# Half of the cached latents turned by transfers within SBUF and VectorE block transposes, with spaced gathers, one rotary product, and another start and end

## The chip, the cores and the metric

One core of one Trainium2 chip runs the whole program in one launch. The metric is the device time in microseconds (us); the number of the kernel before is the median of three runs. A profiled execution of the same program, with a trace of every instruction, is a run of its own with a time of its own.

## What is computed

A decoder trunk of two layers for one prompt of 256 tokens and for 8 sequences that add one token each. The 264 tokens share the weights, so they go through every projection together. Each layer has three branches (gated delta rule, latent attention, mLSTM), a merge and a feed-forward block with a short convolution; a last RMSNorm ends it. The part that the change touches most is the latent attention of the 8 sample sequences over 2048 cached positions each:

```python
q_lat = jnp.einsum('bqhd,chd->bqhc', q_nope, w_uk.reshape(MLA_KV_LORA, MLA_HEADS, MLA_NOPE))
s_past = jnp.einsum('bqhc,bkc->bhqk', q_lat, lat_past) + jnp.einsum('bqhr,bkr->bhqk', q_rope, kr_past)
...
p = jax.nn.softmax(s, axis=-1).astype(lat_past.dtype)
ctx = (jnp.einsum('bhqk,bkc->bqhc', p[..., :past], lat_past)
       + jnp.einsum('bhqk,bkc->bqhc', p[..., past:], c_kv.astype(lat_past.dtype)))
...
y_prompt = rmsnorm(xp, final_norm_g)
y_sample = rmsnorm(xs, final_norm_g)
```

`lat_past` (2048 rows of 128 latents a sequence) and `kr_past` (2048 rows of 32) are gathered through a page table. Everything is float32.

## The kernel before

**Program.** Five engines have streams written out by hand, one function each (sync, tensor, scalar, vector, gpsimd), and wait for one another by semaphores. TensorE's order is the plan: `schedule()` lists every PSUM bank's product in that order and who reads it ("A" ScalarE, "V" VectorE), and the other streams must follow it.

**Weight stream.** SyncE loads the weights in units of 512 KB into a ring of 8 slots (`ring`, line 500). It may issue unit u once TensorE has started unit u - 7 of that count (`w_started`). A unit feeds 8 tiles of 128x128; `weights` (line 547) multiplies each by 264 token columns.

**Pieces.** Projections whose results are needed late (`PIECES`, half a unit each, 4 tiles) fill TensorE's stream while other engines work on the branches: `half(n)` does the next n of them on TensorE, and the same calls in ScalarE's and VectorE's streams evacuate those that are complete. They use two of the eight PSUM banks in turn, so a piece waits for the evacuation of the one before last.

**Pages.** `pages(n)` handles sequence n = 0 to 7 of a layer. `lat[n]` holds its 2048 cached rows, 16 of 128 latents in each partition (1 MB); `key[n]` the rotary keys. Per page:
- TensorE turns the 16 blocks of `lat[n]` by transposes (line 1032) into four banks `ltr`; ScalarE copies two of them to `ltt` and VectorE the other two (line 2052), and VectorE turns `key[n]` by one block transpose (line 2049).
- One piece, then the scores: four products with the latents (line 1039) and four with the rotary keys (line 1042), each into 32 of the 128 output rows. Four pages add up in one bank `ss`.

After four pages `top(g)` finds the maximum, ScalarE takes the exponent (`powers`), `turned(g)` sums, `context(g)` multiplies the probabilities with `lat` untransposed (line 1078), and `combine(g)` (line 1089) sorts the result. Pages 4 to 7 are placed between these steps of group 0.

**Gathers.** GpSimd issues two indirect transfers for each page (`gather`, lines 2338 and 2339). Those of pages 0 to 3 are issued earlier; those of 4 to 7 all together once `pv` is evacuated.

**Other places.** After `os`, one piece and then the products `mn0` (line 833), which wait for VectorE's `ones_column` (line 1894). `outer` (line 847) multiplies 32 rows at a time on four row groups in turn; `mout` (line 900) does so on two. At the start VectorE scales x (line 1553) once `par_loaded` has reached 80: the parameters from SyncE (16) and four tiny transfers to `prow` from ScalarE's queue (64). At the end: sum of squares over the last tile, one product with ones, root, reciprocal over 128x264 (line 2196), eight products on VectorE (line 2199), four stores.

## Time and profile before

| | us |
|---|---|
| median of 3 runs | 1277.28 (1276.53 to 1277.31) |
| profiled execution | 1287.18 |
| its span | 1285.3 |
| TensorE busy | 1258.9 |
| VectorE busy | 546.0 |
| ScalarE busy | 254.3 |
| GpSimd busy | 153.1 |
| read from and written to HBM | 183.9 and 9.3 MB |

The span is divided into what TensorE does and where it waits. The chain of waits follows the work that ended last back from release to release; most of it is TensorE's line 547. A float32 product shows as two passes in the trace, a transpose as one. The rows that matter are given below.

### The profile page before, as it was taken

The page shows a single profiled execution, that of the slowest core. Times are in us where ns is not written, and L with a number is a line of the kernel's source. Part 1 is how long each engine was busy: PE and PEld are TensorE (multiplying, and loading weights), DVE is VectorE, ACT ScalarE, POOL GpSimd, SP SyncE. Part 2 cuts the span into 40 slices and gives each one's busy share as a digit, 9 for nine tenths or more (in the row PEclk, how much of TensorE's full clock was granted, in tenths as well). Part 3 has the DMA queues.
Part 4 walks back from the last instruction along what each step waited for, and adds up shares of the span by engine and source line. Part 5 has one row for each costly group of instructions (what it writes and reads, how often), then busy time and mean ns, then how long its engine had stood idle before and what let it go on. Part 6 is the DMA issues. An engine that isn't in the chain of part 4 may idle for free.

```text
span 1285.3 us, 18245 instructions
## 1 busy us (share of the span) xinstructions
PE 1258.9 (98%) x7278; PEld 1027.3 (80%) x7278; DVE 546.0 (42%) x1372; ACT 254.3 (20%) x648; POOL 153.1 (12%) x210
## 2 busy tenths in 40 slices
PE   7999999999999999999999999999999999999997
PEld 6878777677888888888888787786788888888885
DVE  7975646332135333331178846553311353334212
ACT  3432325222000111110033224342210011111000
POOL 2012442200000000020001035412000000000000
PEclk9999999999999999999999999999999999999999
DMA  9433476522444444464444344745234444444440
GB/s 336 153 99 102 132 249 226 214 82 83 132 153 147 148 148 148 147 218 151 147 152 137 109 129 145 259 164 213 67 99 147 152 145 149 149 149 148 153 133 34
DMA packets 59603, 194.30 MB, mean 151 GB/s; under 512 B 7824, under 2 KB 8112, under 8 KB 56704
## 3 DMA queue, kind: packets, MB, share of 16 engines
q1 hardware_dynamic: 50544, 152.22, 36.6%
q0 software_dynamic: 8768, 40.84, 8.9%
q8 instruction: 58, 0.95, 0.3%
q14 instruction: 25, 0.20, 0.0%
q10 hardware_dynamic: 208, 0.09, 0.0%
HBM read 183.86 MB, written 9.25 MB: 150 GB/s over the span
## 4 chain that ended last, share of the span: by engine, by line
PE 93%; DVE 3%; issue 2%; ACT 1%; POOL 0%; another core or an unknown queue 0%; DMA 0%; ACTq 0%; DVEq 0%; POOLq 0%
PE banks L547 75%; PE banks L1032 3%; PE banks L1039 1%; PE banks L1042 1%; PE banks L938 1%; PE banks L1078 1%; DVE arena L1658 1%; PE banks L966 1%; PE banks L691 1%; PE banks L847 0%; PE banks L982 0%; PE banks L564 0%; DMA arena<-in_par 0%; POOL arena L2282 0%
## 5 line engine op out<-in xcount | busy, mean ns | idle before, releaser
L547 PE MATMUL banks<-arena 128*128 128x264 f32 x4512 | 1032.1, 388 | 7.4 <-DVE arena L1553 6.7
L547 PEld LDWEIGHTS banks<-arena 128*128 128x128 f32 x4512 | 850.7, 190 | 171.8 <-issue 14.3
L1167 ACT ACTIVATE arena<-banks 128x256 f32<-128x256 f32 (+8 forms) x260 | 96.9, 397 | 436.0 <-PE banks L547 293.6
L2153 DVE TENSOR_SCALAR arena<-arena 128x256 f32<-128x256 f32 x44 | 18.2, 414 | 129.9 <-ACT arena L1167 129.7
L2186 DVE SCALAR_TENSOR_TENSOR arena<-banks,arena 128x264 f32<-128x264 f32 x16 | 6.9, 433 | 135.0 <-PE banks L547 135.0
L2364 POOL COPY arena<-arena 128x2 f32<-128x2 f32 x44 | 13.6, 310 | 377.7 <-ACT arena L1167 276.0
L1747 DVE SCALAR_TENSOR_TENSOR arena<-arena,banks 128x264 f32<-128x264 f32 x16 | 6.9, 430 | 73.6 <-PE banks L547 73.6
L1198 ACT ACTIVATE arena<-banks 128x264 f32<-128x264 f32 x32 | 12.5, 391 | 127.4 <-PE banks L547 127.4
L1032 PEld LDWEIGHTS banks<-arena 128*128 128x128 f32 x256 | 28.8, 145 | 7.4 <-issue 7.3
L2052 DVE COPY arena<-banks 128x512 f32<-128x512 f32 x32 | 21.5, 679 | 28.5 <-PE banks L1032 15.7
L1032 PE MATMUL banks<-arena 128*128 128x128 f32 x256 | 32.1, 280 | 0.0
L1479 ACT ACTIVATE arena<-arena 128x256 f32<-128x256 f32 x44 | 18.4, 417 | 66.4 <-DVE arena L2155 66.4
L2160 DVE SCALAR_TENSOR_TENSOR arena<-arena 128x256 f32<-128x256 f32 x44 | 18.7, 426 | 26.8 <-ACT arena L1479 26.6
L2360 POOL DMA_DIRECT2D arena<-in_ffn x2 | 2.9, 1432 | 225.4 <-ACT arena L1167 225.4
L2165 DVE TENSOR_TENSOR arena<-arena,banks 128x256 f32<-128x256 f32 x42 | 17.7, 422 | 26.8 <-PE banks L547 26.6
L2338 POOL DMA_INDIRECT arena<-in_lat,page_row x16 | 15.4, 961 | 88.8 <-ACT arena L1167 67.6
L1039 PE MATMUL banks<-arena 128*32 128x512 f32 x128 | 18.3, 643 | 6.8 <-ACT arena L1167 6.3
L1658 DVE SCALAR_TENSOR_TENSOR arena<-arena 128x256 f32<-128x256 f32 x48 | 23.3, 485 | 1.7
L2155 DVE SCALAR_TENSOR_TENSOR arena<-arena 128x256 f32<-128x256 f32 x44 | 21.5, 490 | 1.6
L2154 DVE SCALAR_TENSOR_TENSOR arena<-arena 128x256 f32<-128x256 f32 x44 | 21.4, 485 | 1.5
L2122 DVE SCALAR_TENSOR_TENSOR arena<-banks,arena 128x264 f32<-128x264 f32 x16 | 6.9, 432 | 34.9 <-PE banks L547 34.9
L2262 POOL TENSOR_TENSOR arena<-arena 128x512 f32<-128x512 f32 x16 | 16.1, 1038 | 37.2 <-DVE arena L1813 37.2
(435 smaller groups left out, 1042.9 us busy)
## 6 DMA issues: line engine op xcount, KB each, us to landing
arena<-in_weights SPq DMA_DIRECT2D x230, 512.0 KB, 3.5
arena<-in_weights SPq DMA_DIRECT2D x112, 256.0 KB, 3.0
arena<-in_s POOLq DMA_DIRECT2D x2, 2048.0 KB, 11.0
out_ss_o<-arena POOLq DMA_DIRECT2D x16, 256.0 KB, 3.0
arena<-in_mla_w POOLq DMA_DIRECT2D x4, 1024.0 KB, 6.8
arena<-in_c POOLq DMA_DIRECT2D x4, 512.0 KB, 5.8
out_sc_o<-arena POOLq DMA_DIRECT2D x16, 128.0 KB, 3.5
arena<-in_x SPq DMA_DIRECT2D x4, 264.0 KB, 5.2
```

Of the source, the lines that this page charges most:

```text
L547: mm = nc.tensor.matmul(dst, ring[:, at_:at_ + 128], rhs[:, j, :], start=(start and j == 0), stop=(stop and j == k - 1))
L1032: mm = nc.tensor.transpose(b[:, q * P:(q + 1) * P], lat[n][:, r_ * P:(r_ + 1) * P], ident)
L1039: nc.tensor.matmul(heads(sb[32 * i:32 * i + 32, :], 32), ql_pad[:, g, s_, :], turned_lat(n)[:, :, 32 * i:32 * i + 32], start=(s_ == 0), st ...
L1167: return A(dst, src, ACT.Copy, scale=scale)
L1479: A(fth[:, j % 3, :], fcv[:, j % 3, :], ACT.Tanh, scale=0.5).then_inc(*up("ffn_tanh"))
L1658: link(stt(cv, ci[:, j, 24 + t:24 + t + TP], w[t], cv, ALU.mult, ALU.add))
L2052: V.tensor_copy(ltt[:, n % 2, i, :], bank("ltr", 4 * n + i)).then_inc(*read("ltr", 4 * n + i))
L2153: link(ts(cv, fc[:, j % 3, 0:TP], w[0], par[:, Q_FB + j:Q_FB + j + 1], ALU.mult, ALU.add))
L2154: link(stt(cv, fc[:, j % 3, 1:1 + TP], w[1], cv, ALU.mult, ALU.add))
L2155: stt(cv, fc[:, j % 3, 2:2 + TP], w[2], cv, ALU.mult, ALU.add).then_inc(*up("ffn_conv"))
L2160: link(stt(cv, fth[:, j % 3, :], 1.0, cv, ALU.add, ALU.mult))
L2165: tt_(hid[:, j, 0:TP], cv, bank("fu", j)[:, 0:TP], ALU.mult)
```

## The change

1. **Latents of sequences 4 to 7.** Their turning leaves TensorE. `lat[n]` is copied into `lat[n - 4]` (free once `context(0)` has read it) by 16 transfers within SBUF for each page, of 32 partitions x 16 x 32 elements (`quarter_of_latents`): 128-byte runs, which swap the four 32-partition groups with the four 32-latent groups. Then VectorE turns each 512 columns by a block transpose of 32x32 blocks, four a page. SyncE issues pages 4 and 6, at two places of the weight stream (`BLOCKS_AT`), ScalarE pages 5 and 7, four transfers ahead of each of eight `half(1)`.
2. **Order.** Pages 4 to 7 follow `combine(0)` and 11 pieces. One more piece stands ahead of `mn0`.
3. **Gathers.** Page 4's is issued as before; those of 5, 6 and 7 each after the transposes of page 1, 2 and 3.
4. **Rotary product.** `qr_pad` is laid out with all heads' 128 columns, so that one product replaces four.
5. **`mout`** uses four row groups; `kvt` and `vd` are filled for all 128 rows by two more products.
6. **Start.** The first unit is loaded in two halves, x's first part on ScalarE's queue, and `par_loaded` no longer includes `prow`.
7. **End.** Sums of squares of all tokens as columns (128x3) by small products, root and reciprocal on these, spread by products into two banks; x was scaled by the gain earlier; VectorE does five tiles and stores go out from SyncE, GpSimd does three tiles and ScalarE issues their stores.

```diff
@@ schedule @@
-    add("mkT", 2); add("mvT", 2); add("sk", 1, "V"); add("mqk", 2, "V"); add("os", 1, "V"); half(1)
+    add("mkT", 2); add("mvT", 2); add("sk", 1, "V"); add("mqk", 2, "V"); add("os", 1, "V"); half(2)
...
@@ sync @@
+            def blocks_of_latents(l, n):
+                sp.wait_ge(*out(l, "cx", 0))
+                sp.wait_ge(*at(l, f"lat_in{n}", 32))
+                for b in range(4):
+                    for q in range(4):
+                        sp.dma_start(*quarter_of_latents(n, b, q)).then_inc(*up(f"lat_blocks{n}", 16))
...
+                if u % UNITS in (BLOCKS_AT, BLOCKS_AT + 1):
+                    blocks_of_latents(u // UNITS, 4 + 2 * (u % UNITS - BLOCKS_AT))
...
+        def quarter_of_latents(n, b, q):
+
+            return (lat[n - 4][32 * q:32 * q + 32, 512 * b:512 * b + 512].rearrange("i (r j) -> i r j", r=NR),
+                    lat[n][32 * b:32 * b + 32, :].rearrange("i (r q j) -> i r q j", r=NR, q=4)[:, :, q, :])
@@ tensor, pages @@
+                    half(1)
+                    if n < 4:
...
+                    else:
+                        pe.wait_ge(*at(l, "lat_turned", 4 * (n - 3)))
...
-                    for i in range(4):
-                        mm = nc.tensor.matmul(sb[32 * i:32 * i + 32, :], qr_pad[:, i, g, s_, :], krt[:, n % 2, :],
-                                              start=False, stop=(s_ == 3), skip_group_check=True)
+                    mm = nc.tensor.matmul(sb, qr_pad[:, g, s_, :], krt[:, n % 2, :], start=False, stop=(s_ == 3), skip_group_check=True)
@@ scalar @@
+                for n in (5, 7):
+                    act.wait_ge(*at(l, f"lat_in{n}", 32))
+                    for b in range(4):
+                        for q in range(4):
+                            nc.scalar.dma_start(*quarter_of_latents(n, b, q)).then_inc(*up(f"lat_blocks{n}", 16))
+                        half(1)
@@ vector, pages @@
+                    else:
+                        dve.wait_ge(*at(l, f"lat_blocks{n}", 256))
+                        for i in range(4):
+                            V.transpose(ltt[:, n % 2, i, :], lat[n - 4][:, 512 * i:512 * i + 512]).then_inc(*up("lat_turned"))
@@ gpsimd @@
-                for n in range(4, NB):
+                gather(4)
+                for n in range(5, NB):
+                    pool.wait_ge(*out(l, "ltr", 4 * (n - 4) + 3))
+                    plain()
                     gather(n)
@@ end of the tensor stream @@
-            pe.wait_ge(last_sum, 7)
-            nc.tensor.matmul(banks[:, 0, 0:TT], ones, nsum, start=True, stop=True).then_inc(last_total, 1)
+            tokens = [slice(0, P), slice(P, TP), slice(TT - P, TT)]
...
+            for b in last_rms:
+                for i, s in enumerate(tokens[:2]):
+                    nc.tensor.matmul(b[:, s], roots[:, i:i + 1].to_broadcast((P, P)), ident, start=True, stop=True, skip_group_check=True)
```

TensorE's stream of layer 1 before, from page 4's transposes to page 6's (L1032 transposes, L547 pieces at 4 products each, L1039 and L1042 scores, L1068 `turned`, L1078 `context`):

```order
L1032 MATMUL banks<-arena 128x128 x16
L547 MATMUL banks<-arena 128x264 x4
L1039 MATMUL banks<-arena 32x512 x4
L1042 MATMUL banks<-arena 32x512 x4
L547 MATMUL banks<-arena 128x264 x4
L1068 MATMUL banks<-arena 128x1
L1032 MATMUL banks<-arena 128x128 x16
L547 MATMUL banks<-arena 128x264 x4
L1039 MATMUL banks<-arena 32x512 x4
L1042 MATMUL banks<-arena 32x512 x4
L1078 MATMUL banks<-arena 32x128 x64
L1032 MATMUL banks<-arena 128x128 x16
```

The same stretch of the changed kernel, from the pieces after `top(0)` to page 5 (L567 pieces, L1095 `turned`, L1105 `context`, L1116 `combine`, L1068 and L1070 scores):

```order
L567 MATMUL banks<-arena 128x264 x12
L1095 MATMUL banks<-arena 128x1
L1105 MATMUL banks<-arena 32x128 x64
L567 MATMUL banks<-arena 128x264 x8
L1116 MATMUL banks<-arena 128x8 x4
L567 MATMUL banks<-arena 128x264 x48
L1068 MATMUL banks<-arena 32x512 x4
L1070 MATMUL banks<-arena 128x512
L567 MATMUL banks<-arena 128x264 x4
L1068 MATMUL banks<-arena 32x512 x4
L1070 MATMUL banks<-arena 128x512
```

The transposes are gone, three, two and twelve pieces stand around `context(0)` and `combine(0)`, and pages 4 to 7 follow one after another.

SyncE's queue of the changed kernel around the two places of the transfers (L518 weights, L501 transfers of pages 4 and 6); before, these were 34 half units in a row:

```order
L518 DMA arena<-in_weights 128x512 x8
L501 DMA arena<-arena 32x16x32 x16
L518 DMA arena<-in_weights 128x512 x2
L501 DMA arena<-arena 32x16x32 x16
L518 DMA arena<-in_weights 128x512 x24
```

Every weight unit behind them waits for `context(0)` and for their issue.

ScalarE's stream of the changed kernel from the exponent of group 0 (L1474) through the copy of the context (L1206), with the transfers of pages 5 and 7 (L1493) between evacuations of pieces (L1237):

```order
L1474 ACTIVATE arena<-banks,arena 128x512
L1237 ACTIVATE arena<-banks 128x264 x2
L1206 ACTIVATE arena<-banks,arena 128x512
L1493 DMA arena<-arena 32x16x32 x8
L1237 ACTIVATE arena<-banks 128x264
L1493 DMA arena<-arena 32x16x32 x8
L1237 ACTIVATE arena<-banks 128x264
L1493 DMA arena<-arena 32x16x32 x8
L1237 ACTIVATE arena<-banks 128x264
L1493 DMA arena<-arena 32x16x32 x8
```

Eight transfers now stand ahead of each of four evacuations.

## Rows read from the trace of the kernel before

**Rows 1.** The page, busy time, share of the span and instructions of each engine
```profile
PE 1258.9 (98%) x7278; PEld 1027.3 (80%) x7278; DVE 546.0 (42%) x1372; ACT 254.3 (20%) x648; POOL 153.1 (12%) x210
```
**Rows 2.** Waits of TensorE: line, released by; us in total, times, longest
```profile
PE banks L547 <- DVE arena L1553: 6.7, 1, 6.7
PE banks L1039 <- ACT arena L1167: 6.3, 2, 3.2
PE banks L833 <- DVE arena L1894: 2.5, 2, 1.2
```
**Rows 3.** Chain of waits, pages 1 to 3 of layer 1: start, us, what
```profile
247.16 3.09 PE banks L1032 x16
...
256.84 2.63 PE banks L1032 x16
...
263.14 1.90 PE banks L1032 x16
265.04 1.78 PE banks L547 x8
266.82 1.02 PE banks L1039 x8
267.84 0.86 PE banks L1042 x8
```
**Rows 4.** Timeline of TensorE, then ScalarE, at page 1: start, us, engine, line
```profile
247.09 1.97 PE L1032 MATMUL banks<-arena 128*128 128x128 f32 x16
...
250.27 0.60 ACT L1167 ACTIVATE arena<-banks 128x512 f32<-128x512 f32 x1 [6.58 <-PE banks L1032]
253.15 0.60 ACT L1167 ACTIVATE arena<-banks 128x512 f32<-128x512 f32 x1 [2.28 <-remote]
```
**Rows 5.** Timeline of GpSimd, first and last of eight gathers
```profile
241.68 0.95 POOL L2338 DMA_INDIRECT arena<-in_lat,page_row  x1 [33.78 <-ACT arena L1167]
...
250.47 0.95 POOL L2339 DMA_INDIRECT arena<-in_key,page_row  x1 [0.30 <-issue]
```
**Rows 6.** Stretch 250 to 260: busy by engine, granted clock, DMA share, GB/s
```profile
250.00:260.00 10.00, 6.84 (x40) 4.07 (x39) 3.52 (x6) 2.39 (x4) 1.12 (x2) 0.83 0.85 349
```
**Rows 7.** VectorE's block transposes: ns min/median/max, first and last start
```profile
L2049 DVE STREAM_TRANSPOSE arena<-arena x16: 687/702/711, 242.0 to 930.7; 128x512 f32<-128x512 f32 x16
```
**Rows 8.** DMA queues (packets, MB, share) at 364:371, 2.3:6.5, all; weight issues; landing
```profile
q0 software_dynamic: 64, 0.18, 15.6%
...
q10 hardware_dynamic: 24, 0.00, 0.3%
...
q1 hardware_dynamic: 50544, 152.22, 36.6%
...
L500 SPq DMA_DIRECT2D arena<-in_weights x342: 327/328/1521, 1.7 to 1246.9; - x171
...
arena<-in_weights SPq DMA_DIRECT2D x112, 256.0 KB, 3.0
```
**Rows 9.** Chain of waits at the outer products of the delta rule and of mLSTM
```profile
152.47 1.07 PE banks L847 x8
...
177.06 1.92 PE banks L900 x8
```
**Rows 10.** Chain of waits at the start and at the end
```profile
2.16 4.07 DMA arena<-in_par
...
6.66 6.73 PE banks L547 x16
...
1254.90 20.14 PE banks L547 x90
...
1277.66 1.81 DVE arena L2196
...
1280.40 2.42 DVE arena L2199 x6
```
**Rows 11.** The page, a group of GpSimd: busy, mean ns of one, idle before
```profile
L2262 POOL TENSOR_TENSOR arena<-arena 128x512 f32<-128x512 f32 x16 | 16.1, 1038 | 37.2 <-DVE arena L1813 37.2
```

More of the change, by code:

```diff
@@ L494, in _ @@
                 if u == 1:
-                    for i in range(1, 4):
+                    for i in range(2, 4):
                         load_x(i)
@@ L543, in weights @@
                         slot = unit % SLOTS
-                        if part == 0:
+                        if unit == 0 and part == 0:
+                            pe.wait_ge(first_half, 16)
+                        elif part == 0 or unit == 0 and part == 4:
                             pe.wait_ge(w_landed[slot], landed[unit])
@@ L1096, in _ @@
                 top(0)
-                pages(4)
-                half(1)
+                half(3)
                 turned(0)
-                pages(5)
                 context(0)
-                pages(6)
-                half(1)
+                half(2)
                 combine(0)
-                pages(7)
+                half(11)
+                for n in range(4, NB):
+                    pages(n)
                 half(2)
@@ L1325, in _ @@
                 A(dm, dm, ACT.Exp, scale=-1.0).then_inc(*up("mdecay_exp"))
-                half(1)
+                half(2)
                 act.wait_ge(*out(l, "mn0"))
@@ L1347, in _ @@
                 act.wait_ge(*out(l, "out", 7))
-                copy(kvt[0:64, :], bank("mkvT")[0:64, 0:P]).then_inc(*read("mkvT"))
+                copy(kvt, bank("mkvT")[:, 0:P]).then_inc(*read("mkvT"))
                 half(3)
@@ L1447, in _ @@
                 powers(0)
-                pages(4)
-                half(1)
-                pages(5)
+                half(3)
                 context(0)
-                pages(6)
-                half(1)
-                pages(7)
+                for n in (5, 7):
+                    act.wait_ge(*at(l, f"lat_in{n}", 32))
+                    for b in range(4):
+                        for q in range(4):
+                            nc.scalar.dma_start(*quarter_of_latents(n, b, q)).then_inc(*up(f"lat_blocks{n}", 16))
+                        half(1)
+                half(5)
+                half(4)
                 half(3)
@@ L2091, in _ @@
                 top(0, 1)
-                pages(4)
-                half(1)
+                half(3)
                 total(0)
-                pages(5)
                 newest(0)
-                pages(6)
-                half(1)
+                half(2)
                 combined(0)
-                pages(7)
+                half(11)
+                for n in range(4, NB):
+                    pages(n)
                 top(1, 2)
@@ L2383, in _ @@
                 close()
+            pool.wait_ge(last_copy, 1)
+            pool.wait_ge(last_scaled, KT)
+            for k in range(5, KT):
+                tt_(hn[:, k, :], raw[:, k, :], rms, ALU.mult).then_inc(last_pool, 1)
         assert not [n for n in SIGNALS if given[n] != L * SIGNALS[n]], given
```

144 lines of the change are left out of this document (87 added, 57 removed).

## The prediction

> **What bounds the kernel now.** I read the page's busy times first: TensorE is busy for 98% of the span [rows 1], so a time that falls off TensorE's stream, or a gap in it that closes, is a gain, and work that moves to another engine costs only where TensorE comes to wait for it. Then the waits of TensorE by who released it [rows 2]: 6.7 us at the start, 6.3 in two waits before page 1's score products, 2.5 in two waits before the products of line 833. The chain of waits then gives the price of every piece of the stream, and the stretches where TensorE itself shows no wait but runs long.
>
> **The profiled execution is not the timed one.** It takes 1287.18 us (span 1285.3), the timed runs 1277.28: 9.9 us apart. The chain shows a place of about that size. An undisturbed page is 1.90 us of transposes, 1.78 of projection, 1.02 and 0.86 of scores, 5.56 in all [rows 3]. Page 1 of layer 1 runs from 247.16 to 256.84, 9.68, and page 2 from there to 263.14, 6.30: 4.86 us too much, and the second wait of the pair [rows 2] stands in layer 2 in the same place, so some 9.7 us in both. What happens there: TensorE's transposes of page 1 start at 247.09, but ScalarE's copy of the first of them is released only at 250.27 and the next at 253.15 by nothing that the profile can name [rows 4]. It is not the data of those transposes that is missing, since they have run. It falls together with eight gathers issued back to back from 241.68 to 250.47 [rows 5], with 349 GB/s on the DMA engines, and the granted clock sinks to 0.83 of the stretch, in part at the 1.2 GHz level, after TensorE's gap [rows 6]. The signal of a finished product arrives late while the memory is saturated. The recording itself may cause that delay, since it has every product to note down just then. That 9.9 and 9.7 agree is my reason to give this the larger chance: the timed runs then have no such stall, and spacing the gathers gains 9.7 us in the profile and nothing in the timed runs. The Trainium skill ("NOTIFIC — the notification-queue block", section 7.1) says that the recorder's inner pipeline holds its producer back rather than lose a record and that the path could throttle an engine; no row here shows that counter, and by that rule the gain would be of the profile alone.
>
> **The change part by part, in timed microseconds.**
>
> *Transposes of pages 4 to 7 off TensorE.* Per layer four groups of 16, 1.80 to 1.90 each (as the row of page 3, 1.90 [rows 3]); 4 x 1.85 x 2 layers = 14.8 gained. They become 16 VectorE block transposes of 128x512 a layer in the place of 8 copies of the same size, each 0.70 [rows 7], and 64 transfers a layer.
>
> *When are they needed?* Call T0 the end of context(0) (the 128 passes of line 1078 in the chain of before). After it TensorE has 2 + 11 pieces, at 20.14/90 x 8 = 1.79 us each [rows 10], some 0.8 of combine, and page 4's own piece: page 4's scores are due at T0 + 26. VectorE reads piece 12 of these at T0 + 22.3, then needs 0.9 for it and 5 transposes x 0.70: done at about T0 + 26.7. So TensorE waits some 0.5 us for page 4, and hardly for pages 5 to 7 (a page takes TensorE 1.79 + 1.9, VectorE 3.5, with two buffers): 1.0 lost in both layers. Page 6's and 7's blocks must have landed by T0 + 31.
>
> *The transfers.* A layer has 64 x 512 = 32768 pieces of 128 bytes, 2048 for each of 16 DMA engines. No row of before has such a transfer. Below: the load of in_ffn is 2816 pieces of 64 bytes in 64 packets; 15.6% of 16 engines x 7 us is 17.5 us, 6.2 ns a piece [rows 8], so 12.7 us a layer. Above: every piece a packet of its own. A packet of 4 to 16 bytes costs 0.3% x 16 x 4.2 us / 24 = 8.4 ns, and bytes cost 36.6% x 16 x 1285.3 us / 152.22 MB = 49 ns per KB, 6.3 for 128 bytes [rows 8]: 14.7 ns, 30.1 us a layer. I take 13, 26.6 us, close to the dear end: q10, of the tiny packets, is ScalarE's queue, which the change uses, and in_ffn comes through GpSimd's. With 3 us for the landing and the two weight units queued between them, all is there by T0 + 30, just within T0 + 31: nothing lost, and at 14.7 ns 2 us a layer. The weight stream behind them on SyncE: units up to seven ahead have been issued, the eighth is needed at T0 + 36. In general a layer loses 2048 p + 3 - 31 us, p the price of a piece.
>
> The Trainium skill speaks both ways ("DMA: Bandwidth & Descriptors"). Its table of specifications has at least 512 bytes for line rate, with a read-modify-write below that; a doubled 14.7 ns would lose 32 us a layer. Its section "Why small descriptors are slow" exempts transfers within SBUF and has 128-byte packets at 78% of link rate, by which a layer's 4 MB would take an estimated 12 us. No row shows either.
>
> *Issuing.* ScalarE issues 32 of these in a layer between evacuations that free the two banks of the pieces. If an issue takes i, its fourth evacuation stands at 32 i + 2.3 and the bank is wanted at T0 + 17: no wait up to 0.46. A weight load, 128 rows, takes 0.328 [rows 8]; if that doesn't depend on the rows, 0.33; if it is all by row, 4 x 0.328 = 1.31 for 512. I take the low end, the row that is nearest in kind, and 0.
>
> *Spaced gathers.* 0 timed, 9.7 in the profile (above); bounds 0 and 9.7.
>
> *A further piece before the products of line 833.* The wait there, 2.5 in two [rows 2], is shorter than the piece (1.79) put ahead of each: 2.5 gained. What is late next: nothing, since the piece is taken from a place with no wait.
>
> *Outer products on four row groups.* L900 with two row groups takes 1.92 for 8 passes, L847 with four 1.07 [rows 9]: 0.85 x 2 = 1.7. Four added products of 128x128 in float32, at twice a transpose's 1.90/16: 0.24 x 4 = 0.9. Net 0.8.
>
> *One rotary product for four.* 8 passes in 0.86 [rows 3] become 2 of 512 columns over the full width. The four ran side by side, so the two take the same; at the rate of the other score rows, 1.02, it would be 16 x 0.16 = 2.6 worse. I take 0.
>
> *Start.* The first product at 6.66 waits for VectorE, which waits for the last of four tiny parameter transfers, issued 2.16 and landed 6.23 [rows 10]. It now waits for the first of them only, for x from ScalarE's queue and for half a weight unit: a 256 KB half lands in 3.0 [rows 8] and is issued near 1.3, so the first product may stand at 4.5. The 16 passes that follow take 6.73, 0.42 each, nearly twice 20.14/90, so they keep their length and move. Gain 2.0; between 0.5, if x's later tiles are late, and 2.3.
>
> *Tail.* From the last pass, 1275.04, to 1285.3 it is 10.3 us: three VectorE steps, a product, a root, a reciprocal over 264 columns of 1.81, eight products of which six take 2.42 up to 1282.8 [rows 10], and 2.5 for the last store. After: two VectorE steps 0.95, small products 0.4, root and reciprocal of three columns 0.4, spreading 0.5, then five products of 0.40 on VectorE beside a copy and three on GpSimd (0.4 + 3 x 0.6, from 1.04 for 512 columns [rows 11]), store 2.5: 7.2. Gain 3.0 (2 to 4).
>
> Sum: 14.8 - 1.0 + 2.5 + 0.8 + 2.0 + 3.0 = 22.1. Timed 1277.28 - 22.1 = **1255**. In the profile 9.7 more: span 1285.3 - 31.8 = 1253.5, about the timed value.
>
> **Rivals.** *B: the stall at page 1 is in the timed runs too.* For it: the late signals stand in the trace with all consequences, clock included. Against: the 9.9 us. It gives 1277.28 - 31.8 = 1245.5. *C: small losses around the blocks.* Issue at 0.6 instead of 0.33 leaves ScalarE 32 x 0.6 + 2.3 - 17 = 4.5 us late a layer, 9 in all: 1264; pieces of 15 to 18 ns give 6 to 18 likewise. For it: deadlines with margins of 1 us. *D, slower than before: the price of a piece.* TensorE stands before page 4's and page 6's scores, and behind the blocks on SyncE's queue the weights. It takes back all 22.1 when 2048 p - 28 = 11, p = 19 ns; at 25 ns it loses 23.2 a layer and the time is 1255 + 46 = 1301. Against it: a 14.7 ns bound put together from the dearest rows; for it: neither row is a transfer from SBUF to SBUF through 32 partitions. ScalarE's issues reach the same point at i = 0.81.
>
> **How the numbers follow.** Forecast (1250 to 1259) 0.48; B (1241 to 1249) 0.22; C (1259 to 1274) 0.15; D 0.11; between C and D, 1274 to 1280, 0.04. The range leaves out D, what lies between and the ends: 1242 to 1272. A measurement of this kernel can tell some 0.2%, 2.5 us: faster 0.86, same 0.03, slower 0.11.
>
> **What would show it.** In the profile of the changed kernel: 128 transposes on TensorE's transpose line instead of 256; page 1 in 5.6 us; no wait at mn0's products; mout's 8 passes in about 1.07; the first product near 4.5 and 7 us from the last pass of the stream to the end; ScalarE's issues at 0.33 to 0.45; the blocks' packets at 13 ns and landed 26 to 30 us after context(0); timed and profiled times within 3 us. A wait of TensorE longer than 1 us before page 4 to 7's scores, or at a piece for weights, refutes the price of the pieces; a profile that stays 10 us above the timed runs refutes the reading of page 1.

## The result: 1300.5 us, slower by 23.5, and the profile after

The changed kernel takes 1300.51 us (median of 1299.38 to 1301.65), the kernel before beside it 1277.04 (1276.53 to 1277.31): a ratio of 1.0183, 95% interval 1.0171 to 1.0195. I had forecast 1255, with a range of 1242 to 1272. The time lies in my rival D, but the price of a piece, D's main mechanism, is not what put it there.

The page of the changed kernel, first row, then the two queues of SyncE and of ScalarE (packets, MB, share of 16 engines):

```profile
PE 1258.9 (97%) x7084; PEld 1024.7 (79%) x7084; DVE 551.7 (42%) x1392; ACT 245.8 (19%) x633; POOL 155.4 (12%) x213
q1 hardware_dynamic: 84192, 155.74, 40.3%
q10 hardware_dynamic: 34432, 4.96, 3.5%
```

TensorE is busy for as many microseconds as before [rows 1], although 128 transposes are gone; slow passes, below, fill their place. Half of the 65536 new packets are on q1, half on q10. TensorE's waits (line, released by; us in total, times, longest) say where it lost:

```profile
PE banks L567 <- ACT arena L1237: 15.3, 4, 4.2
PE banks L567 <- issue: 7.1, 2, 4.6
PE banks L567 <- DMA arena<-in_weights: 5.0, 1, 5.0
PE banks L930 <- DVE arena L2004: 1.5, 2, 0.7
PE banks L1068 <- DVE arena L2109: 1.2, 4, 0.4
```

The two waits of page 1 and those of line 833 [rows 2] are gone, the one at the start is shorter (5.0 for 6.7). New are 22.4 us at line 567, the pieces of projection, three waits a layer, and 1.5 at line 930. The blocks themselves cost 1.2: TensorE hardly ever waits for the scores. In time, TensorE in layer 1 from the end of context(0), 277.5:

```profile
277.39 3.83 PE L567 MATMUL banks<-arena 128*128 128x264 f32 x16
...
281.87 7.37 PE L567 MATMUL banks<-arena 128*128 128x264 f32 x32
292.54 3.83 PE L567 MATMUL banks<-arena 128*128 128x264 f32 x16 [3.31 <-ACT arena L1237]
300.97 3.70 PE L567 MATMUL banks<-arena 128*128 128x264 f32 x8 [4.60 <-issue]
308.63 12.11 PE L567 MATMUL banks<-arena 128*128 128x264 f32 x40 [3.96 <-ACT arena L1237]
321.17 1.06 PE L1068 MATMUL banks<-arena 128*32 128x512 f32 x8 [0.42 <-DVE arena L2109]
```

And ScalarE in the same stretch (L1493 issues a transfer, L1237 reads a finished piece and frees its bank):

```profile
277.53 6.56 ACTq L1493 DMA_DIRECT2D arena<-arena  x8
284.14 0.39 ACT L1237 ACTIVATE arena<-banks 128x264 f32<-128x264 f32 x1 [5.92 <-issue]
284.15 7.89 ACTq L1493 DMA_DIRECT2D arena<-arena  x8
292.10 0.39 ACT L1237 ACTIVATE arena<-banks 128x264 f32<-128x264 f32 x1 [7.57 <-issue]
292.12 8.31 ACTq L1493 DMA_DIRECT2D arena<-arena  x8
300.48 0.39 ACT L1237 ACTIVATE arena<-banks 128x264 f32<-128x264 f32 x1 [7.99 <-issue]
300.50 7.64 ACTq L1493 DMA_DIRECT2D arena<-arena  x8
308.19 0.39 ACT L1237 ACTIVATE arena<-banks 128x264 f32<-128x264 f32 x1 [7.32 <-issue]
```

The two rows of starts interlock. ScalarE reads a piece at 292.10, TensorE goes on at 292.54; ScalarE at 300.48, TensorE at 300.97; 308.19 and 308.63. Between 277.5 and 308.2 ScalarE does nothing but issue, apart from its copy of the context and three reads. One issue lasts 0.95 us on average there (30.4 / 32). What follows each wait is slow too. The stretches by 10 us (busy of TensorE, its weight loads, VectorE, ScalarE, GpSimd; granted clock; DMA share, which passes 1 where packets of two queues overlap; GB/s):

```profile
290.00:300.00 10.00, 3.83 (x16) 2.96 (x16) 0.00 (x0) 0.39 (x1) 0.00 (x0) 1.00 1.49 163
300.00:310.00 10.00, 5.07 (x11) 3.68 (x12) 0.86 (x2) 0.78 (x2) 0.00 (x0) 0.72 1.56 145
310.00:320.00 10.00, 10.00 (x36) 8.02 (x36) 2.75 (x6) 0.39 (x1) 0.00 (x0) 0.77 1.14 292
```

After a stretch in which TensorE was busy for 3.83 of 10 us, the granted clock is 0.72 and then 0.77, so part of these 20 us ran at the 1.2 GHz level. Forty passes take 12.11 where 40 x 20.14 / 90 [rows 10] is 8.95, eight take 3.70 for 1.79: 5.1 us a layer, on top of 11.9 of waits (3.31 + 4.60 + 3.96). Layer 2 shows the same (waits of 3.74, 2.47 and 4.25, together 10.5, and 6.9 of slow passes).

The other places. A page is now (chain of waits: start, us, what; compare [rows 3]):

```profile
247.38 1.75 PE banks L1057 x16
249.13 1.78 PE banks L567 x8
250.91 1.02 PE banks L1068 x8
251.93 1.06 PE banks L1070 x2
...
177.13 1.15 PE banks L924 x8
```

The last row is the outer products, 1.15 for 1.92 [rows 9]. The end of the kernel, from the last pass at 1285.38:

```profile
1287.43 0.18 DVE L2252 RECIPROCAL arena<-arena 128x3 f32<-128x3 f32 x1 [0.86 <-ACT arena L1534]
1287.67 1.22 PE L1174 MATMUL banks<-arena 128*128 128x128 f32 x4 [0.48 <-DVE arena L2252]
1289.45 1.79 DVE L2255 TENSOR_TENSOR arena<-arena,banks 128x264 f32<-128x264 f32 x5 [1.83 <-PE banks L1175]
1291.59 2.14 POOL L2446 TENSOR_TENSOR arena<-arena 128x264 f32<-128x264 f32 x3 [85.83 <-ACT arena L1536]
```

It is 14.5 us from the last pass to the end of the span, 1299.9; it was 10.3. E2, with the same code at the end, has 13.0. The 1.5 between them is the clock: the products that spread the roots (L1174 here) ran at a granted clock of 0.50 from 1287.9 to 1289.9, and at 1.00 in E2:

```profile
1267.08 0.71 PE L1165 MATMUL banks<-arena 128*128 128x128 f32 x4 [0.48 <-DVE arena L2236]
```

### The profile page after: what moved, and what is told of

It is laid out like the page before. It is cut to its first block, busy times and chain, and to the rows that moved or that the text cites. A ratio compares the mean times of both kernels' runs of the same rounds, so it can differ in the third digit from the quotient of the medians.

```text
span 1299.9 us, 17990 instructions
## 1 busy us (share of the span) xinstructions
PE 1258.9 (97%) x7084; PEld 1024.7 (79%) x7084; DVE 551.7 (42%) x1392; ACT 245.8 (19%) x633; POOL 155.4 (12%) x213
## 4 chain that ended last, share of the span: by engine, by line
PE 88%; ACTq 4%; DVE 4%; issue 1%; ACT 1%; DMA 0%; SPq 0%; POOL 0%; POOLq 0%; DVEq 0%
PE banks L567 72%; ACTq L1493 4%; PE banks L1070 1%; PE banks L1105 1%; PE banks L1068 1%; PE banks L1057 1%; PE banks L962 1%; DVE arena L2109 1%; DVE arena L1710 1%; PE banks L990 1%; PE banks L711 1%; PE banks L669 0%; DMA arena<-in_x 0%; PE banks L1006 0%; DVE arena L2004 0%
## 5 line engine op out<-in xcount | busy, mean ns | idle before, releaser
L567 PE MATMUL banks<-arena 128*128 128x264 f32 x4512 | 1044.5, 391 | 28.0 <-ACT arena L1237 15.3
L567 PEld LDWEIGHTS banks<-arena 128*128 128x128 f32 x4512 | 857.9, 192 | 197.4 <-issue 21.9
L1206 ACT ACTIVATE arena<-banks 128x256 f32<-128x256 f32 (+8 forms) x244 | 87.7, 384 | 389.2 <-PE banks L567 292.9
L1799 DVE SCALAR_TENSOR_TENSOR arena<-arena,banks 128x264 f32<-128x264 f32 x16 | 6.9, 430 | 99.6 <-PE banks L567 99.6
L1237 ACT ACTIVATE arena<-banks 128x264 f32<-128x264 f32 x32 | 12.5, 391 | 177.8 <-PE banks L567 120.0
L1794 DVE SCALAR_TENSOR_TENSOR arena<-arena,banks 128x264 f32<-128x264 f32 x16 | 6.9, 429 | 30.3 <-PE banks L567 30.3
L2109 DVE STREAM_TRANSPOSE arena<-arena 128x512 f32<-128x512 f32 x32 | 19.6, 671 | 0.0
L2105 DVE COPY arena<-banks 128x512 f32<-128x512 f32 x16 | 11.1, 692 | 18.9 <-PE banks L1057 18.9
L1068 PE MATMUL banks<-arena 128*32 128x512 f32 x128 | 17.2, 610 | 1.2 <-DVE arena L2109 1.2
```

What stands on the lines that cost most here:

```text
L567: mm = nc.tensor.matmul(dst, ring[:, at_:at_ + 128], rhs[:, j, :], start=(start and j == 0), stop=(stop and j == k - 1))
L1068: nc.tensor.matmul(heads(sb[32 * i:32 * i + 32, :], 32), ql_pad[:, g, s_, :], turned, start=(s_ == 0), stop=False, skip_group_check=True)
L1206: return A(dst, src, ACT.Copy, scale=scale)
L2109: V.transpose(ltt[:, n % 2, i, :], lat[n - 4][:, 512 * i:512 * i + 512]).then_inc(*up("lat_turned"))
```

## The experiments

Sixteen experiments on four chips. Beside them the kernel before takes 1283.9 to 1288.1 us in every one of 36 executions, not 1277; E1 bears on that. So I compare mostly kernel with kernel. E3, E5, E6 and E9 leave transfers out or copy other shapes, so that their output is another, and have one execution each; the others have four to ten.

**E1, the gathers alone**

```diff
-                for n in range(4, NB):
+                gather(4)
+                for n in range(5, NB):
+                    pool.wait_ge(*out(l, "ltr", 4 * (n - 4) + 3))
+                    plain()
                     gather(n)
```

> The kernel before with one edit: the last three pairs of gathers of a layer wait for TensorE's transposes of pages 1, 2 and 3, as in the changed kernel. Theory (the stall at page 1 belongs to the recorded execution): in the trace page 1 takes about 5.6 us instead of 9.68, the span falls by some 9.7 us to about 1275.6, and the timed runs do not move: 1277 within 1.5 us, so that profiled and timed execution agree within 2 us. Rival B (the stall is in every execution): the timed runs fall to about 1267.5.

Measured: 1276.89 (1276.62 to 1277.28), before 1285.82 beside it, ratio 0.9934 (0.9917 to 0.9950); span 1274.7. Page 1 in its trace:

```profile
247.97 1.95 PE L547 MATMUL banks<-arena 128*128 128x264 f32 x8
249.85 1.09 PE L1039 MATMUL banks<-arena 128*32 128x512 f32 x8
```

No wait before the scores. Spacing the gathers removes the stall, and what I expected of this kernel came: page 1 undisturbed, the span at 1274.7, the time at 1277. What I had not expected is the kernel before beside it, 1285.8 and not 1277. That could mean that the stall depends on the chip and not on the recording. But each of the 36 executions, like every execution of E1 and of the changed kernel, has a span and a granted clock of its own on record, as the profiled execution has; the four at 1276.5 to 1277.3 have neither. "A recorded execution stalls" and "these four chips stall, and the one of my prediction doesn't" both fit all of this, and no run separates them. The second needs the profiled execution behind the prediction, 1287.18, to have run on such a chip, which isn't recorded.

**E13, the changed kernel again**, beside the kernel before on such a chip

> The changed kernel as it is, timed beside the kernel before on a chip of the experiments, where the kernel before took 1286 to 1287 and not 1277. Theory (before's stall at page 1 is in its timed runs on these chips, and the changed kernel has no such stall anywhere): 1300 as before, so the loss here is 13 to 15 us instead of 23.5. Rival (these chips are slower for every kernel by 0.7%): 1309.

Measured: 1299.64 (1297.72 to 1301.49) against 1287.04: ratio 1.0095 (1.0079 to 1.0110). The changed kernel takes what it took (1300.51), so these chips are not slower for every kernel; the loss is 12.6 us against executions of the kernel before at 1287, and 23.5 against those at 1277.

**E2, everything but the blocks** (pages 4 to 7 turned by TensorE in their old places, no transfers within the chip, all other hunks of the change)

> The changed kernel without its main part: pages 4 to 7 are turned by TensorE where they were before, no blocks are transferred; the gathers, the rotary product, the further piece, the outer products on four row groups, the start and the tail are as in the changed kernel. Theory (the blocks cost all of the loss, and the smaller edits give less than I took): start -1.0, the wait at line 833 -2.5, outer products +1 to +2, rotary product 16 x 0.2 less what the transposes give back, 0 to +3.2, tail +3.7 by what the two traces show, gathers 0: 1277 to 1282. The blocks then carry 18 to 24 of the 23.5 us. Rival (the smaller edits are worth what I predicted, -8.3): 1269, and the blocks carry 31. Rival (they are themselves the loss): above 1290.

Measured: 1279.98 (1279.90 to 1280.15), 3.1 above E1 and within the expected 1277 to 1282. The rest of the change, for which I had 8.3 of gain, loses 3.1; the blocks lose 19.7 (1299.6 - 1280.0), where I had 13.8 of gain.

**E3, pages 5 and 7 left out**

```diff
-                    act.wait_ge(*at(l, f"lat_in{n}", 32))
                     for b in range(4):
-                        for q in range(4):
-                            nc.scalar.dma_start(*quarter_of_latents(n, b, q)).then_inc(*up(f"lat_blocks{n}", 16))
                         half(1)
```

> The changed kernel without ScalarE's 32 transfers a layer (the blocks of pages 5 and 7 are left out, VectorE transposes what lies in their buffers, so the output for sequences 5 and 7 is another). SyncE still issues its 32. Theory (an issue lasts as long as the DMA engines need to take up its pieces, both queues sharing them at 16.2 ns a piece): SyncE's issues fall from a median of 0.90 us to 32 x 16.2 ns = 0.52, or to the 0.6 of the first ones, whichever is longer; a layer's 16384 packets are done some 18 to 20 us after context(0); no wait of TensorE is left at the pieces, and the span falls by about 2 x 17 to 1266 to 1270. Rival (an issue has a fixed price of its own, whatever else is queued): SyncE's issues stay at 0.9. Rival (the loss comes from the packets under way, not from ScalarE's issues): TensorE's waits at the pieces stay in part.

Measured: 1265.99. No wait of TensorE at the pieces is left. SyncE's issues now (ns min/median/max), and the queue in 9 us of them, 280 to 289:

```profile
L501 SPq DMA_DIRECT2D arena<-arena x64: 591/630/1551, 278.3 to 922.0; - x64
q1 hardware_dynamic: 6602, 0.82, 58.5%
```

In the changed kernel the same line has 591/900/1909. From context(0) to page 4's scores it is 26.5 us (277.52 to 304.04), in the changed kernel 43.7 (277.5 to 321.17): the 17 us a layer. SyncE's issues fell with ScalarE's gone, so an issue has no fixed price of 0.9. A piece costs 58.5% x 16 x 9 / 6602 = 12.8 ns here. The gain of the transposes is whole: 1280.0 - 1266.0 = 14.0.

**E6, pages 4 and 6 left out**

```diff
-                if u % UNITS in (BLOCKS_AT, BLOCKS_AT + 1):
-                    blocks_of_latents(u // UNITS, 4 + 2 * (u % UNITS - BLOCKS_AT))
```

> The mirror of the run without pages 5 and 7: SyncE's 32 transfers a layer are left out (VectorE transposes what lies in the buffers of pages 4 and 6, so their output is another), ScalarE issues its own 32 with nothing beside them. Theory (0.71 us an issue, as SyncE's took when alone, is enough to hold ScalarE): its fourth evacuation of these comes 32 x 0.71 + 2.3 = 25 us after context(0) where TensorE wants the bank at 17: 8 us a layer, 16 in all above the 1266 of the mirror run, 1280 to 1284. Rival (ScalarE is late only since both queues together fill the DMA engines): no wait at the pieces, 1266 to 1269.

Measured: 1291.85. ScalarE's issues, and TensorE's waits:

```profile
L1491 ACTq DMA_DIRECT2D arena<-arena x64: 607/657/1928, 277.6 to 937.7; - x64
PE banks L565 <- ACT arena L1235: 9.5, 4, 3.4
PE banks L565 <- issue: 7.6, 2, 3.9
```

ScalarE's fourth read of a piece comes 25.6 us after context(0) (25 expected). The waits are 17.1 (16 expected). What I left out again is the clock: the whole is 25.9 above E3, so some 9 us follow from the slow passes after the waits (granted clock 0.53 from 300 to 310). Issues of 0.66 us in the median and 0.79 on average (25.4 / 32) are enough to lose 25.9 of the 33.6 us, with half of the pieces and only SyncE's weight loads beside them.

**E5, the same transfers in pieces of 2 KB**

```diff
-            return (lat[n - 4][32 * q:32 * q + 32, 512 * b:512 * b + 512].rearrange("i (r j) -> i r j", r=NR),
-                    lat[n][32 * b:32 * b + 32, :].rearrange("i (r q j) -> i r q j", r=NR, q=4)[:, :, q, :])
+            return lat[n - 4][32 * q:32 * q + 32, 512 * b:512 * b + 512], lat[n][32 * b:32 * b + 32, 512 * q:512 * q + 512]
```

> The changed kernel with the same 64 transfers a layer, the same queues and the same 64 KB each, but each of 32 rows is copied as one piece of 2 KB instead of 16 pieces of 128 bytes (the blocks lie wrong, so the scores of pages 4 to 7 are another computation). Theory (the number of pieces sets both how long an issue lasts and how long the DMA engines work): 128 pieces an engine a layer instead of 2048, an issue of 0.35 us or less, all blocks landed about 16 us after context(0), at 49 ns a KB some 13 us of transfer; no wait of TensorE at the pieces: 1266 to 1270, as with pages 5 and 7 left out. Rival (bytes or the number of transfers decide): issues stay near 0.9 to 1.0, the time near 1300.

Measured: 1282.14.

```profile
L1492 ACTq DMA_DIRECT2D arena<-arena x64: 521/614/1775, 277.8 to 929.0; - x64
PE banks L566 <- ACT arena L1236: 7.5, 2, 4.4
PE banks L566 <- issue: 3.1, 2, 1.6
```

Half of my theory fell: a sixteenth of the pieces, and an issue still lasts 0.61. The other half held: the pieces' crowd on the DMA engines had raised it to 0.87, and without them 17.5 us of the loss go (1299.6 - 1282.1).

**E9, other shapes**

```diff
+            k = 128 * (4 * b + q) if n % 2 == 0 else 512 * b
+            return lat[n - 4][:, k:k + (128 if n % 2 == 0 else 512)], lat[n][:, k:k + (128 if n % 2 == 0 else 512)]
...
-                        for q in range(4):
+                        for q in range(1):
```

> The changed kernel with its transfers within SBUF in two other shapes (plain copies, so the scores of pages 4 to 7 are another computation): SyncE's 32 a layer copy 128 rows of 512 bytes each, 64 KB as before; ScalarE's are 8 a layer of 128 rows of 2 KB, 256 KB each, the shape of a weight load but from SBUF instead of memory. What is measured is how long an issue lasts: 32 rows as 512 pieces of 128 bytes took 0.71 alone, 32 rows of 2 KB 0.66, a weight load of 128 rows 0.33 to 0.43. Theory (it is the source within SBUF that makes an issue dear): 0.65 or more in both shapes. Rival (it is the shape, 32 rows on one side): 0.33 to 0.43 in both. With ScalarE's eight issues at either price there is no wait at the pieces: 1266 to 1269.

Measured: 1265.90, and the issues of ScalarE (128 rows of 2 KB), then of SyncE (128 rows of 512 bytes):

```profile
L1493 ACTq DMA_DIRECT2D arena<-arena x16: 472/566/1216, 277.7 to 910.9; - x16
L501 SPq DMA_DIRECT2D arena<-arena x64: 471/602/1975, 278.3 to 921.4; - x64
```

A load of weights with the same rows takes 0.33 [rows 8], and it does so in this trace too (median 328 ns, at most 725). What differs is that the source lies in SBUF: 0.57 to 0.60. So the number of rows or pieces hardly counts for the issue; whether both ends lie in SBUF does. (I had said 0.65 or more; it is a little less.) With eight issues a layer instead of 32, ScalarE delays nobody.

**E4, GpSimd issues pages 5 and 7**

```diff
+                pool.wait_ge(*out(l, "cx", 0))
+                for n in (5, 7):
+                    pool.wait_ge(*at(l, f"lat_in{n}", 32))
...
+                            dma(*quarter_of_latents(n, b, q)).then_inc(*up(f"lat_blocks{n}", 16))
```

> The changed kernel with ScalarE's 32 transfers a layer issued by GpSimd, which has nothing to do there; same transfers, same order, complete computation. From the trace of before a GpSimd issue lasts 0.52 to 0.55 us, one of 2816 pieces 1.43: some 0.7 for 512 pieces. Theory (ScalarE held by its issues is what makes TensorE wait, the pieces themselves arrive almost in time): TensorE's waits at the pieces vanish; the blocks land at context(0) + 35 at most, 1 to 4 us late a layer for pages 6 and 7: timed 1266 to 1273. If GpSimd's way of writing its packets gives 6.2 ns for a piece, as in_ffn's 64-byte pieces had, all are in by + 28 and it is 1264 to 1267. Rival (the price of the pieces is the cause, whoever issues them): 1285 or above, with TensorE waiting before the scores of pages 4 to 7 instead.

Measured: 1279.77 (1279.47 to 1281.91). TensorE's waits:

```profile
PE banks L1068 <- DVE arena L2106: 15.3, 4, 6.6
```

ScalarE was the cause of the waits at the pieces: they are gone. The rest is worse than I expected (1266 to 1273), though below the rival's 1285. GpSimd's 32 issues (0.67 each) are out in 20.6 us, and while they run SyncE's first 16 take 25.9 us; page 4, wanted first, is the one that suffers. TensorE stands 6.6 us before page 4's scores. GpSimd's transfers show on a queue of their own as packets of 2 KB (274 to 318):

```profile
q0 software_dynamic: 1024, 2.10, 39.7%
```

That is 39.7% x 16 x 44 us / 1024 = 0.27 us a packet, 17 ns for 128 bytes: no cheaper than the pieces of the other queues.

**E8, both queues in order of need** (of each page eight transfers by SyncE, eight by GpSimd, page after page)

> The changed kernel with the blocks in order of need: of each page's 16 transfers SyncE issues eight and GpSimd eight, page 4 first, GpSimd starting a page when SyncE's half of the page before has landed; ScalarE issues none. Complete computation. Theory (the DMA engines take up 512 pieces of a page in 8.3 us at 16.2 ns, and only the order and ScalarE's issues lost time): pages 4, 5, 6, 7 have landed 11, 19, 28 and 36 us after context(0), where VectorE wants them at 22 to 26, 29, 33 and 36: 1265 to 1269. Rival (the drain itself is too slow, by the same 16 to 17 ns, since GpSimd's and SyncE's transfers don't overlap well or weights behind SyncE's half come late): 1272 to 1280.

Measured: 1283.31 (1279.88 to 1286.16), above even the rival's range. The theory fell. Page 7's blocks landed 44 us after context(0), TensorE waited 7.7 us for them in one layer, and the weights behind SyncE's share came 3.7 us late. The packets of the two queues took 92% of the DMA engines' time in the 34 us from 278 (shares of 55.0 and 36.9), so there was little slack that an order could use. It is not a clean test of order, though: this kernel holds GpSimd back until SyncE's half has landed, and GpSimd stands idle for 6.5, 2.5 and 6.6 us between its groups.

**E7, the tail without GpSimd** (base: E2)

```diff
-            for k in range(5):
+            for k in range(KT):
                 tt_(hn[:, k, :], raw[:, k, :], last_rms[0], ALU.mult).then_inc(last_norm, 1)
...
-            for k in range(5, KT):
-                tt_(hn[:, k, :], raw[:, k, :], rms, ALU.mult).then_inc(last_pool, 1)
```

> The kernel with all edits but the blocks (1280.0), its last products changed: VectorE makes all eight instead of five, ScalarE's copy and GpSimd's three products go, the last store waits for VectorE. Theory (GpSimd's own end, 8.07 us from the start of its late products, ends the span, 3.7 us after the last store has landed): from the last pass to the end 9 to 9.8 us instead of 13.0, 1276 to 1277. Rival (the stores set the end, GpSimd's drain only stands beside them): three products more on VectorE, 1.0, take the place of GpSimd's 2.1, 1279 to 1280.

Measured: 1275.59 (1274.99 to 1275.82), 4.4 below E2. From the last pass to the end it is 10.0 us (1263.9 to 1273.9) instead of 13.0, though the roots were spread at a granted clock of 0.52 here; at full clock, in E10's trace, it is 9.3. Another 0.9 lies at the start, where the tiles of x happened to land earlier than in E2's trace. The trace has for the last instruction of GpSimd's program, a drain (start from the end of the span, us):

```
changed, E2, E3, E5, E6, E13:  -8.30  8.07 us     E9:  -8.31  8.08 us
E4:  -4.67  3.74 us     E8:  -4.68  4.40 us
before, E1, E7:  none of GpSimd in the last 16 us
```

In the changed kernel it runs from 1291.6 to 1299.6, 3.8 us beyond the last store's landing at 1295.8. It begins with GpSimd's three late products. Why it is shorter in E4 and E8, where GpSimd had issued 64 transfers more, I can't tell; there the stores end the span.

**E10, no blocks, and two edits undone** (base: E7 without the outer products on four row groups and without the single rotary product)

> No blocks: gathers in order, the further piece, the start, and the tail on VectorE as in the run without GpSimd; the outer products on four row groups and the single rotary product are undone. Theory (both cost time: the outer products 0.96 a layer, from the time between the products of the normalization and those of the output in the two traces, the rotary product 0.05 a page): 1275.6 - 1.9 - 0.8 = 1272.9. Rival (they are worth what I predicted, 0.8 and 0): 1276.4.

Measured: 1272.88 (1272.24 to 1273.54), 2.7 below E7, as expected. The outer products (E2, then E10; from the first product of their operands to the next stage):

```profile
173.16 0.27 PE L906 MATMUL banks<-arena 128*64 128x128 f32 x1
...
178.07 1.14 PE L919 MATMUL banks<-arena 32*128 32x512 f32 x8
...
181.92 1.97 PE L925 MATMUL banks<-arena 128*32 128x128 f32 x64 [0.73 <-DVE arena L1992]
```

```profile
172.50 0.27 PE L906 MATMUL banks<-arena 128*64 128x128 f32 x1
...
176.38 1.99 PE L915 MATMUL banks<-arena 32*128 32x512 f32 x8
...
180.27 1.97 PE L921 MATMUL banks<-arena 128*32 128x128 f32 x64
```

8.76 us against 7.77. The faster products (1.14) send TensorE into a wait for VectorE that reads their results (0.73), and the added products cost another 0.9. The rotary product was not tested by itself.

**E14, without the new start** (base: E10)

> The kernel without blocks of 1272.9, with the start as in the kernel before (one load of x and one whole unit first, VectorE waiting for all five parameter transfers). Theory (the later tiles of x decide when the first normalization is through, with either start; the steady stream began at 12.8 to 13.7 us in the traces of both): 1272.9 within 1. Rival (the new start is worth the 2.0 that I predicted): 1274.9.

Measured: 1273.23 (1272.97 to 1273.40): the start is worth 0.35, less than the four executions of E10 differ (1.3).

**E12, two pages through blocks, all by SyncE** (base: E10; pages 4 and 5 stay with TensorE)

> The same with pages 6 and 7 alone turned through blocks, all 32 transfers issued by SyncE. Complete computation. Theory: SyncE alone needs 23 us for them at 0.71 us an issue, with no wait of TensorE, as in the run without pages 5 and 7: 4 groups of 1.85 less, 7.4, less 0.5 for VectorE: 1272.9 - 6.9 = 1266. Rival (what is left of the contention still costs): 1268 or more.

Measured: 1270.03 (1269.47 to 1271.60), 4 too much. Its waits name VectorE, `PE banks L1069 <- DVE arena L2108: 4.4, 2, 2.2`.

**E16, the same one piece earlier**

```diff
-                half(13)
+                half(12)
                 for n in range(6, NB):
                     pages(n)
```

> Two pages through blocks again, pages 6 and 7 one piece earlier in the order. Theory (the 2.2 us wait a layer before page 6's scores came from VectorE, which read the piece just ahead before it could transpose; a piece earlier that one is ScalarE's to read, and the wait falls to the 0.4 of the other runs): 1270.0 - 3.6 = 1266.4. Rival (the wait was for the blocks): the wait grows by 1.8 and the time stays at 1270 or above.

Measured: 1265.86 (1265.39 to 1266.63), before 1287.04 beside it: ratio 0.9838 (0.9825 to 0.9851). The wait was VectorE's order, not the blocks. This is the best kernel of the study, 11.2 us under even the 1277.04 of my prediction's runs. Its stretches after context(0) (284.0 here) have TensorE full, the clock whole and the DMA engines at two thirds:

```profile
290.00:300.00 10.00, 10.00 (x46) 8.55 (x45) 0.00 (x0) 1.18 (x3) 0.00 (x0) 1.00 0.61 117
300.00:310.00 10.00, 10.00 (x46) 8.51 (x46) 4.35 (x9) 0.39 (x1) 0.00 (x0) 1.00 0.70 108
```

**E11 and E15, three pages through blocks** (page 4 stays with TensorE). E11: SyncE issues 5 and 7, GpSimd 6. E15: GpSimd 5 and 7, SyncE 6.

> As the kernel without blocks just named, but pages 5, 6 and 7 turned through blocks (page 4 stays with TensorE): SyncE issues 16 transfers each for pages 5 and 7, GpSimd 16 for page 6, ScalarE none. Complete computation. Theory (no engine that TensorE waits for is held by issues, and 1536 pieces an engine at 13 to 16 ns, 20 to 25 us, are done before the pages are wanted): 6 groups of 1.85 less for TensorE, 11.1, less 1.0 for VectorE: 1272.9 - 10.1 = 1262.8. Rival (GpSimd's transfers take the engines from SyncE's and the weights, as with the blocks in order): 2 to 6 us a layer late, 1267 to 1275.

> Three pages through blocks again, with the queues exchanged: GpSimd issues pages 5 and 7, SyncE only page 6, so that the weights stand behind 16 transfers instead of 32. Theory (in the run with SyncE on pages 5 and 7 the weights came late, 6.1 us of TensorE's waits and as much of half clock as follows; with SyncE free some 26 us after context(0) instead of 32 they come in time, and 1536 pieces are done by + 25): 1262 to 1265. Rival (page 7 or the weights are late all the same, since the DMA engines have the same work): 1268 to 1272.

Measured: 1271.24 (1269.93 to 1273.23) and 1277.83 (1277.30 to 1278.52). In both the rival's mechanism won, in E15 by more than its range (to 1272). The waits are now for weights (E11, then E15):

```profile
PE banks L570 <- DMA arena<-in_weights: 11.0, 3, 4.9
PE banks L570 <- DMA arena<-in_weights: 15.4, 3, 5.6
```

About 4.9 of each is the start. No wait of more than 0.2 us for VectorE is left at these pages, so it isn't E12's loss again. SyncE's first 16 transfers take 19.1 us beside 16 of GpSimd's and 26.2 beside 32, and the weights stand behind them in SyncE's queue. The more GpSimd issues, the later they come. Two pages by the one queue beat three by two.

## Why the prediction was wrong, point by point

**The step that failed is "Issuing".** I had taken 0.33 us for ScalarE's issues, the price of a weight load, as "the row that is nearest in kind", and 0 for the loss. An issue of a transfer within SBUF takes 0.57 to 0.66 in the median where the DMA engines aren't crowded (E9, E5, E3, E6), whatever its pieces, and 0.87 to 0.90, 0.95 on average, while two queues crowd them. My own rule for the rest was right: no wait up to 0.46, the fourth evacuation at 32 i + 2.3. With 0.95 it gives 32.7 against a bank wanted at 17, 15.7 late a layer (31.0 in the trace, since the reads overlap the issues). The trace has 11.9 of waits plus 5.1 of slow passes, 17.0, in layer 1 and 10.5 plus 6.9 in layer 2. Both make 34, which is what E3 gives back (1299.6 to 1266.0). I had even priced it: D with "ScalarE's issues reach the same point at i = 0.81". I gave that no chance of its own beside the price of a piece; with a bound from 0.33 to 1.31 and a threshold of 0.46, most of the interval lost time.

**The piece** was right alone: 13 ns forecast, 12.8 measured (E3). Together the two queues moved 11880 packets in 12 us (280 to 292), 12 x 16 / 11880 = 16.2 ns, above my end of 14.7. The blocks were down some 35 us after context(0), not 30. In the changed kernel this is hidden behind ScalarE's delay; E4 and E8 show it as the next limit.

**Issues moved to another engine.** The Trainium skill ("Perfetto Trace Analysis", section "DMA Optimizations") says that balancing DMAs over SyncE, ScalarE and GpSimd may help when descriptor generation is the bottleneck. On ScalarE it did not help here: the engine that issues is lost to TensorE for 0.95 us each time. The Trainium skill ("DMA: Bandwidth & Descriptors", section "Issuing engines are not separate DMA queues") says that all of them share the same 16 DMA engines, and that the time to issue is usually small relative to the transfer. The first half fits this case (16 transfers of SyncE take 10.7 to 11.9 us alone, 19.1 and 26.2 beside GpSimd's). On the second the measurement decides: SyncE issues for 0.63 us (E3) where 32 pieces at 12.8 ns keep a DMA engine for 0.41, though a transfer lands only 2.3 us after its issue. Of the two ways in which my prediction had the page speak, neither came: no run has a doubled 14.7 ns, and a layer's pieces take 2048 x 12.8 ns = 26 us and not the estimated 12. Whether part of the 12.8 is a read-modify-write, no run shows.

**Slow passes after a wait** were in no term. The gaps of 2.5 to 4.6 us cost about half as much again (5.1 for 11.9 in layer 1, 6.9 for 10.5 in layer 2); the granted clock fell to 0.72 and 0.77 behind them.

**Transposes off TensorE**: 14.8 less 1.0 forecast, 14.0 measured (E3 against E2; in E3 TensorE waits at most 0.4 us before the scores).

**Gathers**: 0 for the timed kernel held in the runs of my prediction, and 9.7 in the profile (E1's span is 10.6 under that of the kernel before). Whether my reason was right is open. I read a difference of 9.9 us between a profiled and a timed execution as the effect of recording; E1 shows the same 9 us beside it, but between executions that all have a recorded span (see E1). If the recording is not the cause, the 0 was luck.

**Line 833**: 2.5 forecast. E10 is 4.0 below E1; less 0.35 for the start and 1.0 for the tail (9.3 in its trace, 10.2 in E1's) 2.7 remain, about as forecast.

**Outer products and rotary product**: +0.8 and 0 forecast, together -2.7 measured (E10). I had found the saving (0.8 in the row) but asked only for TensorE: the products' reader, VectorE, became late, and the added products delayed their stage by 0.93 a layer where I had 0.9 for both. The rotary product is 1.06 for 0.86, within the worse end that I had named; the transposes before it went from 1.90 to 1.75.

**Start**: 2.0 forecast (0.5 to 2.3), 0.35 measured. The first product came 1.7 us earlier, but the later tiles of x landed at 6.6 and 8.0 us, and the steady stream began at 12.72 for 13.68. Even that is no gain: with the old start it began at 12.77 in E1, with the new one at 13.75 in E2. I had named this as the low end and not followed it through the later tiles.

**Tail**: 3.0 of gain forecast, a loss of 2.8 (E2) to 4.2. Spreading the roots took 1.1 at full clock (E2) and 1.84 at half (1287.61 to 1289.45) for my 0.5, and GpSimd's drain, in no term, came on top. Without GpSimd it is 10.0 (E7) to 9.3 (E10), a gain of 0.2 to 1.0. My terms for the new tail also add up to 6.95, not 7.2.

Summed from E1 by differences of runs (so the sum must come out; what it shows is the shares): rest +3.1, transposes -14.0, issues and crowd +33.6 (1299.6 - 1266.0): 1276.9 + 22.7 = 1299.6.

**Open** is whether the stall at page 1 comes with the recording or with the chip, and what sets the length of GpSimd's drain.

## What to carry to other kernels

Before an engine that frees buffers is given DMAs to issue, multiply: number of issues by the price of one of just this kind, and compare with the time until the first buffer is wanted; if no row has that kind, take the threshold, not the friendliest row. A transfer moved to another engine still shares the DMA engines and delays what is queued behind it, so the useful amount here was what one queue could carry in the slack: half of the work was worth 7 us (E16 against E10), all of it cost 20 with ScalarE issuing half of it, and gave nothing with GpSimd in ScalarE's place (E4, 1279.8 for 1280.0). And a gain on the bounding engine counts only when the next reader of its result keeps up.

## What the runs showed of the hardware that I had not expected

- An issue of a transfer within SBUF lasts 0.57 to 0.66 us on SyncE or ScalarE with 32 to 512 pieces of any shape tried, against 0.33 for a load from memory with 128 rows; with both queues full it rises to 0.87 to 0.90 (medians).
- Pieces of 128 bytes take a DMA engine 12.8 ns with one queue, 16.2 with two.
- GpSimd's transfers hold SyncE's up more than ScalarE's do: 16 of SyncE's take 11 us alone, 15 beside ScalarE's, 26 beside 32 of GpSimd's.
- GpSimd's final drain lasts 8.07 or 8.08 us in seven traces (3.74 and 4.40 in two others), counted from the start of its late products, and can end the span.
- The kernel before takes 1277 us in four executions and 1284 to 1288 in 36 others. In the traced one the difference is a stall of TensorE, and spacing eight gathers removes it (E1); what decides whether it comes is open.
